# Expert tokens and ways back made one expert at a time, and three more weight tiles loaded ahead

## The reference, cut to what matters

```python
def expert_choice_ffn(h, w_router, w_gate, w_up, w_down):
    affinity = jax.nn.softmax((h @ w_router).astype(jnp.float32), axis=-1)
    top_val, top_idx = lax.top_k(affinity.transpose(0, 2, 1), cap)      # cap = 32 of 256 tokens
    xe = jax.vmap(lambda hb, ib: hb[ib])(h, top_idx)
    act = jax.nn.silu(jnp.einsum('becd,edf->becf', xe, w_gate)) * jnp.einsum('becd,edf->becf', xe, w_up)
    ye = jnp.einsum('becf,efd->becd', act, w_down) * top_val[..., None].astype(h.dtype)
    return jax.vmap(lambda yb, ib: jnp.zeros((s, d), yb.dtype).at[ib.reshape(-1)].add(yb.reshape(-1, d)))(ye, top_idx)
```

## Time and profile before

| | |
|---|---|
| median of 3 runs | 2147.92 us (2146.86 to 2149.06) |
| the profiled execution | 2145.48 us |
| its span in the profile | 2143.7 us |
| busy: PE, DVE, ACT, POOL | 1734.5, 401.5, 293.0, 19.0 us |
| moved by the DMA engines | 558.66 MB, mean 261 GB/s |
| granted TensorE clock, mean | 0.91 of 2.4 GHz |

### The profile page before, as it was taken

The page is one execution under the profiler, slowest core; times in us unless marked ns, Lnnn a source line. Parts: engine busy times, 40 slices in busy tenths (PEclk is TensorE's granted clock), DMA queues, the critical chain, the costliest instruction groups (busy, mean ns, idle before and its releaser), DMA issues. The chain is left out here.

```text
span 2143.7 us, 25348 instructions
## 1 busy us (share of the span) xinstructions
PE 1734.5 (81%) x11074; PEld 1029.8 (48%) x11074; DVE 401.5 (19%) x701; ACT 293.0 (14%) x480; POOL 19.0 (1%) x40
## 2 busy tenths in 40 slices
PE   6999998999999999988999796656655666566665
PEld 4857865888688648878786431111111111111111
DVE  1425422232100022355443210000000000000001
ACT  2231313241100011220230110000000000000001
POOL 0000000000000000000000000000000000000000
PEclk9999999999999999999999798788888878888877
DMA  9531371344554223402415599999999999999997
GB/s 318 214 118 46 113 275 40 120 158 153 208 164 148 81 89 129 147 2 51 156 71 236 200 426 430 428 429 428 428 429 428 429 428 429 429 428 429 428 429 334
DMA packets 120007, 558.66 MB, mean 261 GB/s; under 512 B 15544, under 2 KB 50429, under 8 KB 95229
## 3 DMA queue, kind: packets, MB, share of 16 engines
q1 hardware_dynamic: 117193, 547.97, 64.0%
q10 hardware_dynamic: 2740, 9.59, 1.2%
HBM read 556.49 MB, written 1.05 MB: 260 GB/s over the span
## 5 line engine op out<-in xcount | busy, mean ns | idle before, releaser
L3329 PE MATMUL ps<-ring,xn 128*32 128x512 f32 x2048 | 320.4, 757 | 213.2 <-DMA ring<-in_w_exp_up 111.6
L3329 PEld LDWEIGHTS ps<-ring,xn 128*32 128x32 f32 x2048 | 62.0, 124 | 458.1 <-DMA ring<-in_w_exp_up 181.1
L3349 PE MATMUL ps<-ring,hT 128*32 128x512 f32 x1024 | 170.9, 802 | 103.1 <-DMA ring<-in_w_exp_down 94.9
L360 PE MATMUL ps<-hT,ring 128*128 128x256 f32 x1072 | 239.2, 385 | 4.8 <-PEq L1063 2.8
L360 PEld LDWEIGHTS ps<-hT,ring 128*128 128x128 f32 x1072 | 206.4, 193 | 36.8 <-issue 5.1
L886 PE MATMUL ps<-hT,ring 128*128 128x256 f32 x768 | 179.0, 383 | 0.0
L2110 PE MATMUL ps<-hT,ring 128*128 128x256 f32 x704 | 155.2, 384 | 1.8 <-PEq L729 1.8
L886 PEld LDWEIGHTS ps<-hT,ring 128*128 128x128 f32 x768 | 141.2, 190 | 19.8 <-issue 1.7
L2110 PEld LDWEIGHTS ps<-hT,ring 128*128 128x128 f32 x704 | 135.8, 193 | 21.0 <-issue 2.1
L3349 PEld LDWEIGHTS ps<-ring,hT 128*32 128x32 f32 x1024 | 32.1, 129 | 223.1 <-DMA ring<-in_w_exp_down 159.5
L3427 DVE TENSOR_TENSOR hT<-hT,ps 128x512 f32<-128x512 f32 x16 | 11.0, 688 | 571.8 <-PE ps L3329 566.7
(11 more groups left out here) (541 smaller groups left out, 1421.3 us busy)
## 6 DMA issues: line engine op xcount, KB each, us to landing
ring<-in_w_exp_up SPq DMA_DIRECT2D x64, 2048.0 KB, 26.4
ring<-in_w_exp_gate SPq DMA_DIRECT2D x64, 2048.0 KB, 25.7
ring<-in_w_exp_down SPq DMA_DIRECT2D x64, 2048.0 KB, 26.0
ring<-in_w_in SPq DMA_DIRECT2D x28, 2048.0 KB, 7.9
ring<-in_w_ffn_in SPq DMA_DIRECT2D x11, 2048.0 KB, 8.8
ring<-in_w_in SPq DMA_DIRECT2D x6, 1536.0 KB, 6.7
ring<-in_w_ada SPq DMA_DIRECT2D x4, 2048.0 KB, 18.7
ring<-in_w_out SPq DMA_DIRECT2D x4, 2048.0 KB, 13.7
```

Of the source, the lines that this page charges most:

```text
L360: last = nc.tensor.matmul(k.ps[:, 2 * slot + n // 2, (n % 2) * S:(n % 2 + 1) * S], wt[:, c, n * P:(n + 1) * P], src[:, c, 0:S], start=c == ...
L3329: last = nc.tensor.matmul(k.ps[32 * j:32 * j + 32, bank, :], xe[:, 2 * n + cc, :], slot(q, EFF)[:, cc, j * TILE:(j + 1) * TILE], start=n = ...
L3349: last = nc.tensor.matmul(k.ps[32 * i:32 * i + 32, Y + h, :], act_t[:, i, j, :], slot(q, D)[:, i, h * BANK:(h + 1) * BANK], start=j == 0, ...
```

## The change

Expert e's products gather the 32 tokens of expert e + 1 between their tiles (two chunks behind each of the four pairs of gate and up tiles) and turn expert e's way before the down products. `xeT` and `back` are gone, and with them their part of `tok` and `chan`, and the four tables `four_times`. The constants still in use at the end are moved to the front of their tensor. What is free then is the `Annex`: tiles 6, 7 and 8 of expert 0 go to `constants`, `chan` and `tok`, and are loaded in `third_merge`. All later tiles go to slot (q - 3) % 6. Expert 15 is no longer in the loop on PE and DVE.

```diff
-    for n in range(4):
-        tables[f"four_times{n}"] = p == CAP * n + f % CAP
+    lasting = ("ident", "four_idents", "eps", "slot_number")
+    order = (*lasting, *(name for name in tables if name not in lasting))
...
+LASTING_CONSTANTS = 2 * CAP + P + 1
...
-        self.constants = sb("constants", width)
+        self.constants = sb("constants", max(width, LASTING_CONSTANTS + SLOT))
...
-def third_merge(k, m, ahead):
+def third_merge(k, m, ahead, annex):
...
             issue(k, sp, m.loads[3:])
-            issue(k, sp, ahead)
+            issue(k, sp, ahead[0:1])
+            annex.load(sp, 6)
+            issue(k, sp, ahead[1:4])
+            annex.load(sp, 7)
+            sp.wait_ge(m.merged, m.before["merged"] + DC // 2)
+            annex.load(sp, 8)
+            issue(k, sp, ahead[4:])
...
-                norm_scalar(k, act, m, st, t, junk)
+                norm_scalar(k, act, m, st, t, k.ps[:, 2:3, :])
...
+class Annex:
+    def __init__(self, k, tiles):
+        chan = k.chan[:, :, :].rearrange("p c s -> p (c s)")[:, 0:SLOT]
+        self.places = {6: k.constants[:, LASTING_CONSTANTS:LASTING_CONSTANTS + SLOT], 7: chan, 8: k.tok[:, 0:SLOT]}
+        self.landed = {q: k.sem(f"annex{q}_landed") for q in self.places}
+        self.done = k.sem("annex_done")
+        self.tiles = tiles
+
+    def load(self, sp, q):
+        sp.dma_start(self.places[q], self.tiles[q](0)).then_inc(self.landed[q], 16)
...
+    def ring_place(q, opening):
+        at = q if opening and q < RING else q - extra
+        return at % RING, at // RING
...
             with sp.Fori(0, EXP - 1) as e:
-                for q in range(RING, n_tiles + RING):
-                    u, turn_of_ring = q % RING, q // RING
-                    load(sp, e if q < n_tiles else e + 1, q % n_tiles, e * first + (base[u] + 1 + turn_of_ring))
-            for q in range(RING, n_tiles):
-                load(sp, EXP - 1, q, (EXP - 1) * first + base[q % RING] + 1 + q // RING)
+                for at in range(RING, n_tiles + RING):
+                    u, q = at % RING, at + extra
+                    load(sp, e if q < n_tiles else e + 1, q % n_tiles, u, e * first + (base[u] + 1 + at // RING))
+            for at in range(RING, n_tiles - extra):
+                u = at % RING
+                load(sp, EXP - 1, at + extra, u, (EXP - 1) * first + base[u] + 1 + at // RING)
...
         @block.gpsimd
+            def hot(e):
+                nc.gpsimd.tensor_copy(hot_next, one_hot[:, :, bass.ds(e * CAP, CAP)]).then_inc(hot_ready, 1)
+            def four_copies(e):
+                for t in range(TT):
+                    last = nc.gpsimd.tensor_copy(copies[:, t, :].rearrange("p (i n) -> p i n", i=4), over(weighted[:, t, bass.ds(e * CAP, CAP)], 4))
+                last.then_inc(copies_ready, 1)
             nc.gpsimd.memset(zeros, 0.0).then_inc(zeroed, 1)
+            hot(1)
+            pool.wait_ge(weights_ready, 1)
+            four_copies(0)
+            with pool.Fori(1, EXP - 1) as e:
+                pool.wait_ge(gathered, e + 1)
+                hot(e + 1)
+                pool.wait_ge(way_turned, e)
+                four_copies(e)
...
         @block.tensor
+            def gather(hot, chunks):
+                for c in chunks:
+                    for t in range(TT):
+                        last = nc.tensor.matmul(k.ps[:, GATHERED, c * CAP:(c + 1) * CAP], k.xs[:, t, c::DC], hot[:, t, 0:CAP], start=t == 0, stop=t == TT - 1)
+                return last
+            gather(one_hot, range(DC)).then_inc(gathered, 1)
...
+            def turn_way(e):
+                pe.wait_ge(copies_ready, e + 1)
                 for t in range(TT):
+                    last = nc.tensor.transpose(k.ps[:, GATE, t * P:(t + 1) * P], copies[:, t, :], k.const("ident"))
+                last.then_inc(way_turned, 1)
...
-                        if opening:
-                            gather(q)
+                        release(last, q, opening)
+                    if n < DC // 2 and not closing:
+                        if n == 0:
+                            pe.wait_ge(hot_ready, e + 1)
+                            pe.wait_ge(y_copied[1], e + 1)
+                            if opening:
+                                pe.wait_ge(xe_ready, 1)
+                        last = gather(hot_next, (2 * n, 2 * n + 1))
+                        if n == DC // 2 - 1:
+                            last.then_inc(gathered, 1)
                 if opening:
-                    turn_weights()
+                    clear_sums()
                 pe.wait_ge(hidden, e + 2)
...
                 last.then_inc(turned, 1)
+                turn_way(e)
                 pe.wait_ge(act_ready, e + 1)
...
+                        if j == 0 and h == 1 and not closing:
+                            pe.wait_ge(xe_ready, e + 2)
...
-                    if opening:
-                        spread_ways(2 * j)
-                        spread_ways(2 * j + 1)
-                if opening:
-                    clear_sums()
...
-            expert(0, True)
-            with pe.Fori(1, EXP) as e:
-                expert(e, False)
+            expert(0, opening=True)
+            with pe.Fori(1, EXP - 1) as e:
+                expert(e)
+            expert(EXP - 1, closing=True)
...
         @block.vector
+            def tokens(n):
+                dve.wait_ge(gathered, n + 1)
+                nc.vector.tensor_tensor(xe, k.ps[:, GATHERED, 0:DC * CAP].rearrange("p (c n) -> p c n", c=DC), along(k.row_gain[:, :], CAP), ALU.mult).then_inc(xe_ready, 1)
+            def way_back(e):
+                dve.wait_ge(way_turned, e + 1)
+                nc.vector.tensor_copy(way, k.ps[:, GATE, 0:S]).then_inc(way_ready, 1)
...
+            with dve.Fori(1, EXP - 1) as e:
                 up(e)
+                tokens(e + 1)
+                way_back(e)
                 result(e)
```

More of the change, by code:

```diff
@@ L830, in norm_scalar @@
         act.wait_ge(m.added, m.before["added"] + 2 * t + h + 1)
-        k.achain(k.nc.scalar.activation(junk[:, t, cols], k.x[:, t, cols], ACT.Square, accum_out=st.sums[:, 2 * t + h:2 * t + h + 1]))
+        k.achain(k.nc.scalar.activation(junk[:, t, cols] if junk.shape[1] == TT else junk[:, 0, :], k.x[:, t, cols], ACT.Square, accum_out=st.sums[:, 2 * t + h:2 * t + h + 1]))
         if h == 0:
@@ L3124, in expert_tiles, with expert_choice @@
     return tiles + [rows_down(j) for j in range(EFF // TILE)]
-def expert_choice(k, tiles, out):
+def expert_choice(k, tiles, annex, out):
     nc = k.nc
     tok = k.tok
-    xeT = tok[:, 0:4096].rearrange("p (c n) -> p c n", c=DC)
     one_hot = tok[:, 4096:5120].rearrange("p (t n) -> p t n", t=TT)
@@ L3143, in expert_choice, with load @@
     first = n_tiles // RING
+    extra = len(annex.places)
     refills = k.sem("refills")
-    def load(sp, e, q, before):
-        u = q % RING
+    def load(sp, e, q, u, before):
         sp.wait_ge(k.tile_done[u], before)
@@ L3207, in expert_choice @@
     xe = xn[:, D:D + DC * CAP].rearrange("p (c n) -> p c n", c=DC)
-    turned_w = tok[:, 6144:6144 + D].rearrange("p (g s) -> p g s", g=4)
-    way = tok[:, 7168:7168 + S]
+    copies = tok[:, 6144:6144 + TT * P].rearrange("p (t n) -> p t n", t=TT)
+    hot_next = tok[:, 6400:6400 + TT * CAP].rearrange("p (t n) -> p t n", t=TT)
+    way = tok[:, 7424:7424 + S]
     GATE, UP, TURNED, Y = 4, 5, 6, 6
+    GATHERED = Y + 1
     GATES, NJ = DC // 2, EFF // TILE
@@ L3228, in ways_added, with tile_is_done @@
         engine.wait_ge(way_used, 2 * TT * (EXP - 1) + 2 * t + h + 1)
[L3229 to L3235, removed]
+    gathered, hot_ready = k.sem("tokens_gathered"), k.sem("tokens_hot_ready")
+    weights_ready, copies_ready, way_turned = [k.sem(f"ways_{what}") for what in ("weights_ready", "copies_ready", "turned")]
+    def ring_place(q, opening):
+        at = q if opening and q < RING else q - extra
+        return at % RING, at // RING
+    def tile_is_done(engine, e, q, opening=False):
+        if opening and q in annex.places:
+            engine.wait_ge(annex.done, sorted(annex.places).index(q) + 1)
+            return
+        u, turn_of_ring = ring_place(q, opening)
+        engine.wait_ge(k.tile_done[u], e * first + (base[u] + 2 + turn_of_ring))
     with nc.Block() as block:
@@ L3268, in _ @@
+            pool.wait_ge(way_turned, EXP - 1)
+            four_copies(EXP - 1)
         @block.tensor
         def _(pe):
[L3270 to L3273, removed]
+            def gather(hot, chunks):
[3 more added lines that the diff above has]
+                return last
@@ L3309, in clear_sums, with slot, landed, release @@
                     nc.tensor.matmul(k.ps[:, b, :], zeros[:, 0:P], zeros, start=True, stop=True, skip_group_check=True)
-            def slot(q, width):
-                u = q % RING
+            def slot(q, width, opening):
+                if opening and q in annex.places:
+                    return annex.places[q].rearrange("p (c n) -> p c n", n=width)
```

(27 more changed lines are left out.)

98 lines of the change are left out of this document (22 added, 76 removed).

## The result

The changed kernel takes 2132.90 us (median of 4 runs, 2131.42 to 2134.26), the kernel before 2148.49 us in the same comparison; the ratio is 0.9928 with a 95% interval of 0.9911 to 0.9945, or 15.6 us. The profiled execution took 2133.09 us with a span of 2131.3. (The ratio is the changed kernel's time over the time of the kernel before, both run in the same comparison.)

What follows compares the result with a forecast made beforehand. The prediction took the kernel to be bound by its stream of refill transfers. Three tiles fewer (14.7 us) and smaller constants (0.3) gave 15.0 us off the median of 2147.9, so 2132.9 us, range 2130.0 to 2138.0.

Steps and rivals of the forecast that it cites:

- The stream of refills sets the end, 4.894 us a tile: Refill transfers during the experts: three tiles fewer at 4.894 us each, 14.7 us less.
- The three fit into idle time: Transfers before the first refill: the three tiles need 14.7 of 44 us of idle engine time, cost 0.
- The opening: Expert 0, from 1216.8 us: the stream of refills doesn't run dry; cost 0, up to 5 us as the bound.
- The counted margin of 4.5 us: Expert 0: first ring slot released again near 1243.5 us, while six refills keep the stream busy until about 1248 us.
- Inside the experts: Each expert's period: PE busy 41 to 45 us of 58.7, the added gather hidden under the stream, cost 0.
- The cover of at least 13 us: Each expert's period: at least 13 us of PE idle time remain after the added gather and transposes.
- The rival that PE becomes the bound: Inside the experts: with the clock at 0.5 PE needs 62.3 us an expert, 2183 us in all; chance 0.03.
- The tail: Products and adds behind the last tile: unchanged, taken at 0, bounds 0 and +5 us.
- Expert 15 outside the loop: Last expert: PE fetches fresh code while the engines are full; cost 0, bound +5 us.
- the constants: Transfer of the constants: 262 kB less, gain 0.3 us, bounds 0 and 0.6.

Runs made afterwards that it cites:

- the kernels with no and one tile: Changed kernel with the annex emptied, or keeping tile 6 alone: 2146.42 us and 2141.42 us.
- the rows in order: Changed kernel with the normed rows stored in the order in which the gather reads them: 2128.91 us, ratio 0.9888 to 0.9933.
- the experiment: Changed kernel with the clearing of the sums in expert 0 done three times: 2137.48 us, ratio 0.9930 to 0.9964.
- 16.2 us more of gather: Changed kernel with each gather of the next expert's tokens in experts 1 to 14 done three times: 2133.23 us, ratio 0.9909 to 0.9951.
- the fivefold gather: Changed kernel with each gather of the next expert's tokens in experts 1 to 14 done five times: 2316.39 us, ratio 1.0753 to 1.0800.
- the latter in one run: Changed kernel with rows stored in the gather's order and each gather in experts 1 to 14 done nine times: 2395.01 us.

## Why the prediction was right, point by point

*The number.* That the median came out at the forecast to a tenth is luck. The interval of the ratio stands for 11.8 to 19.1 us; the 15.0 us were taken from a median of 2147.9 and the 15.6 from one of 2148.5; and behind the mark the traces show 14.0. What is right is the mechanism and the size of its main term.

*The stream of refills sets the end, 4.894 us a tile.* Right, and shown by the kernels with no and one tile: 14.0 us behind the mark for three, 4.73 for one. Forecast were 14.7. The missing 0.6 us lie, as far as the runs tell, in the opening: with the rows in order, from the first refill on, the stream is 899.49 us long, 14.6 below the 914.09 of before; in the changed kernel it is 900.04.

*The three fit into idle time.* Right: the transfers went out at 1130.1, 1156.2 and 1157.3 us, and the first refill is no later. The slack in this was the idle stretch before 1217 us, which remains.

*The opening.* Right in its verdict, wrong in a term. I put 8 gather products at 0.9 us, by L345 at full clock; they take 2.02. The 7.79 us for 32 in the first gather were put down to the lower clock, so that the full clock seemed to promise half. But its loads take 0.335 us each with their stride of eight values, and L3283, which loads the same rows at full clock, showed 0.312 us in the trace of before: with this stride the full clock gives back nearly nothing. Side by side, the 32 take 7.00 us at the lower clock and 8 of them 1.08 at full. The timeline of the changed kernel's opening:

```profile
1218.09 2.09 PE L3309 MATMUL ps<-tok,xs 128*128 128x32 f32 x8
1220.11 3.64 PE L3355 MATMUL ps<-ring,xn 128*32 128x512 f32 x32
...
1236.78 3.68 PE L3324 MATMUL ps<-hT 128*128 128x512 f32 x8
```

The slot's second release came at 1245.81 us instead of 1243.5. Four gathers cost 4.5 us more than counted, and other terms less: two tiles follow each other in 3.57 us, not 3.84, and transposes and copy took 1.3 us, not 2. The counted margin of 4.5 us was, by the experiment, some 0.9. The forecast held because the error was smaller than the margin, and by a us only.

*Inside the experts.* One period, from 1293.94 to 1352.70 us, answers to the earlier trace rows:

```profile
L3355 PE MATMUL ps<-ring,xn 128*32 128x512 f32 x128 | 20.8, 782 | 8.4 <-DMA ring<-in_w_exp_up 5.6 <-DMA ring<-in_w_exp_gate 2.9
L3385 PE MATMUL ps<-ring,hT 128*32 128x512 f32 x64 | 9.9, 757 | 6.5 <-DMA ring<-in_w_exp_down 5.9 <-ACT hT L3411 0.5
L3309 PE MATMUL ps<-tok,xs 128*128 128x32 f32 x32 | 8.3, 405 | 0.0
L3395 PE MATMUL ps<-xn,tok 128*128 128x512 f32 x8 | 4.5, 706 | 0.0
```

PE is busy some 44.6 us of this period (with 1.1 for the transposes), inside the forecast's 41 to 45, and still waits for tiles in both groups. The gather in it takes 8.3 us, though, and I had bounded it by 3.74 and 7.79; it is the other products, slightly cheaper than before, that keep the sum inside. The cover of at least 13 us is real: 16.2 us more of gather didn't move the median, and cost 1.7 us behind the mark.

*The rival that PE becomes the bound.* It didn't happen, but my argument against it was wrong. I wrote that the clock fell only where PE waited for tiles, and that a PE that is late isn't idle; the fivefold gather shows 0.74 with PE busy for 806 of 810 us. The trace of before had a sign of it in its first gather:

```profile
1204.90:1212.60 7.70, 7.70 (x32) 7.60 (x32) 0.00 (x0) 0.00 (x0) 0.43 (x1) 0.50 0.23 70
```

PE is busy for all of these 7.70 us, and the clock stays at 0.50. The Trainium skill's "TensorE: Matmul & The Clock Gate", section "HAM oscillation — how this bites in real kernels", has short groups of products fall back to the lower clock because of the waits for transfers between them. That fits the kernels with waits (0.81 and 0.84), but not this fall without a wait. What takes the clock down in a long gather stays open; it isn't the layout of the weights. With a gather somewhere between three and five times the length the rival would have come true.

*The tail.* Taken at 0 with bounds 0 and +5: in the profiled execution the last tile ran at the lower clock (3.64 for 1.92 us) and from its start to the span's end it was 14.6 us for 12.5, +2.1. Thus the two spans differ by 12.4 us, the last products by 14.5 and the medians by 15.6.

*Expert 15 outside the loop, and the constants.* In the stretch from 1300 us on no wait of PE is longer than 3.0 us, and all but 7.9 us of its waits are for tiles. The constants no longer hold up the narrow products: their weight loads start 15.36 us behind the first products of the wide group ahead of them (L363) for 15.67 before, the 0.3 forecast. Nothing of it can be told in the time.

## What to carry to other kernels

Where a chain of waits alternates between a little work and a full queue of transfers, count the transfers left once the stream starts, and the moment it starts: every tile that fits into idle time ahead of it, and every us by which the first slot is released earlier, comes off the end, as long as the engines' work stays under the stream. Then look for the one place where that queue nearly runs dry, here the first expert, since an earlier start is worth no more than what its refills can keep up. When a term is borrowed from a row of like shape, compare how the operands lie, too; and test a cover by repeating what lies under it, as here three and five times, rather than by counting it.

## What the runs showed of the hardware that was not expected

- A load of 128 x 128 float32 weights with a stride of eight values takes 0.335 us at the lower clock and 0.312 to 0.335 at full, and 8 load and multiply pairs take 2.02 to 2.09 us at full clock; side by side they take 1.08. At the lower clock the gain is small, 7.00 for 7.79 us over 32.
- The granted clock falls though the profile shows PE busy throughout: from 0.98 to 0.50 within 9.7 us of products of 32 columns behind 128 x 128 weights, and to 0.74 on the mean over 810 us, for strided and for side-by-side weights alike (the latter in one run). In the first gather it stays at 0.50 for 7.70 us of the same products.
- VectorE writes 128 x 1024 values in an order with a stride of 128 values in 1.33 instead of 0.75 us.
